# Folding squares ahead of the column sums and transposing 128x128 whole in a decoder trunk

## The chip, the cores and the metric

The kernel runs on one core of one Trainium2 chip. The metric is the device time of the whole program in microseconds (us). Three timed runs of the kernel before gave 1185.15, 1185.39 and 1186.02 us; their median is 1185.39 us.

## What is computed

One layer of a decoder trunk over 256 tokens of width 1024, float32: a mixer (sparse attention of 8 heads in 2 groups beside a short gated convolution), cross-attention to 256 memory rows, and a mixture of 32 experts. Cut to what the change touches:

```python
def compress_blocks(t, pos_emb, w1, b1, w2):          # t: keys or values, (B, S, G, 64)
    idx = jnp.arange(nc)[:, None] * CMP_STRIDE + jnp.arange(CMP_LEN)[None, :]
    blk = t[:, idx] + pos_emb[:, None, :]
    blk = jnp.moveaxis(blk, 3, 2).reshape(B, nc, G, CMP_LEN * dh)
    return jax.nn.gelu(blk @ w1 + b1) @ w2
...
sc = jnp.einsum('bsghd,bcgd->bghsc', qg, kc) * scale
p_cmp = jnp.where(cmask, masked_softmax(sc, cmask), 0.0)
o_cmp = jnp.einsum('bghsc,bcgd->bsghd', p_cmp, vc)
...
o = jnp.concatenate([rmsnorm(o_nsa, g_nsa_out), rmsnorm(o_conv, g_conv_out)], axis=-1)
return o @ w_mix_out
```

## The kernel before

The order of the work on each engine is written out by hand, with semaphores between the engines. The program has three stages. The first (to about 187 us) is the mixer. The second (to about 267 us) is the cross-attention and the router. The third runs through the 32 experts; each takes six loads of 2 MB of weights into a ring of 11 slots (line 497), 403 MB in all. The first 11 of these loads are gated one by one by steps of the second stage, because the slots hold data of the stages before; each later one waits until a slot is freed.

The mixer's middle is a loop over eight rounds n = 0 to 7: t = n // 4 is the half of the tokens, j = n % 4 a head of each group. In a round TensorE makes the scores (L1708), VectorE masks them and takes the maximum (`mask_max`, L1221 and L1222), ScalarE takes the exponentials (`exps`, L766), VectorE weighs them (`weigh`, L1228 to L1234), TensorE transposes them (`p_transposes`, by the helper `tr`, L1570) and ScalarE copies them out (`pt_out`, L777). Between these steps TensorE multiplies "units" (L1590 to L1592): chunks of the memory's keys and values, whose weights ScalarE (L655) and VectorE (L1024) have split into a high and a low part.

The steps of the change lie around and inside these rounds:

- `cmp_transposes` (L1684) turns the keys, then the values, of the compression into PSUM banks 6 and 4, before round 0. Each piece of 128 tokens by 64 columns is a multiplication by the identity, made twice so that both halves of the 128 partitions hold a copy. `blocks` (L1160, VectorE) reads them.
- `cmp_p_transposes` (L1799, round 3) turns the compressed probabilities `Pcf`, 16 pieces of 32 columns. `cmp_scores` and `cmp_weigh` on VectorE (L1195 to L1209) fill `Pcf`; `cmp_out` (L794, ScalarE) copies the result out; `pv(0)` (L1813, L1817) uses it in round 4.
- `column_sums` (L1728) sums squares `sq` over partitions by multiplying with a column of ones, four chunks for each half of the tokens. `conv_sums` runs in round 5, on squares that ScalarE writes before round 0 (L747). `o_sums` runs after the rounds, between `mix_out(0, 0)` and `mix_out(1, 0)` (L1826), on squares by `o_square` (L815). ScalarE takes its root (L857), and VectorE scales the attention's part into `H` with it (L1246).
- On GpSimd (POOL), `weight_low` (L573) makes the low part of the output weights in four pairs of subtractions, in rounds 4 to 7. After them the queue waits for the second stage (L586).

## Time and profile before

| what | value |
|---|---|
| median of three runs | 1185.39 us |
| span of the profiled execution | 1185.6 us |
| PE busy (multiplications) | 1117.9 us, 94% |
| PE weight loads | 498.0 us, 42% |
| VectorE, ScalarE, GpSimd busy | 319.6, 233.6, 36.3 us |
| moved by DMA | 445.50 MB, mean 376 GB/s |

No other time of the profiled execution than its span is given; the span lies within the spread of the three runs, so span and time are taken as the same here. A weight load (PEld) runs beside the multiplication before it, and each multiplication needs one, so the starts of the weight loads show the pace of TensorE; the ends of multiplications in the profile are modelled. A float32 multiplication shows as two instructions, a transposition through `tr` as one.

### The profile page before, as it was taken

To read this page: it belongs to the slowest core of one execution; us is meant where nothing else is said; L and a number is where in the kernel's file an instruction comes from. 1 tells how busy PE (TensorE), PEld (TensorE's weight loads), DVE (VectorE), ACT (ScalarE), POOL (GpSimd) and SP (SyncE) were. 2 spreads that over 40 slices of the span, in tenths; PEclk is the share of its full clock that TensorE was granted. 3 is DMA by queue.
4 is the path that set the end of the run, shared out by engine and by line. 5 is a ranking of instruction groups with operands and counts; after the bars stand their busy time and mean duration, and the time that the engine had idled before them with its cause. 6 is when DMAs were issued, how large, how long until landed. Compare 5 with 4: busy or idle time off the path is not lost.

```text
span 1185.6 us, 12841 instructions
## 1 busy us (share of the span) xinstructions
PE 1117.9 (94%) x5460; PEld 498.0 (42%) x5461; DVE 319.6 (27%) x719; ACT 233.6 (20%) x460; POOL 36.3 (3%) x35
## 2 busy tenths in 40 slices
PE   8999999999999999999999998999999989999896
PEld 7887678753333333333333333333333333333332
DVE  6787665233111111221111111111111111111112
ACT  6575665341100000110010000000000000000002
POOL 0000240220000000000000000000000000000000
PEclk9999999999999999999999999999999999999999
DMA  9915336769999999999999999999999999999995
GB/s 361 353 46 185 100 143 263 273 269 426 425 426 430 426 430 426 428 426 428 426 430 427 427 428 428 427 428 426 430 427 427 428 427 428 428 427 427 428 426 215
DMA packets 44586, 445.50 MB, mean 376 GB/s; under 512 B 6096, under 2 KB 10288, under 8 KB 19728
## 3 DMA queue, kind: packets, MB, share of 16 engines
q1 hardware_dynamic: 42784, 444.38, 90.0%
q8 instruction: 44, 0.72, 0.3%
q10 hardware_dynamic: 1744, 0.28, 0.1%
q14 instruction: 14, 0.11, 0.0%
HBM read 443.60 MB, written 1.05 MB: 375 GB/s over the span
## 4 chain that ended last, share of the span: by engine, by line
PE 59%; DMA 35%; DVE 2%; ACT 2%; issue 0%; SPq 0%; DVEq 0%; ACTq 0%
PE ps L2074 19%; DMA R<-in_w_gate_up 16%; PE ps L2083 11%; DMA R<-in_w_down 4%; DMA MK<-in_w_gate_up 4%; PE ps L1570 4%; DMA A<-in_w_gate_up 4%; DMA XMT<-in_w_gate_up 4%; DMA XM<-in_w_gate_up 4%; PE ps L2103 4%; PE ps L2050 3%; PE ps L1590 3%; PE ps L1592 3%; PE ps L1591 3%; PE ps L1934 2%; PE ps L1826 2%
## 5 line engine op out<-in xcount | busy, mean ns | idle before, releaser
L2074 PE MATMUL ps<-R,convT 128*64 128x512 f32 x1104 | 246.4, 594 | 17.4 <-DMA R<-in_w_gate_up 17.4
L1471 DVE TENSOR_SCALAR A<-ps 128x512 f32<-128x512 f32 x30 | 20.8, 692 | 645.1 <-PE ps L2074 645.1
L2074 PEld LDWEIGHTS ps<-R,convT 128*64 128x64 f32 x1104 | 76.7, 137 | 173.7 <-issue 135.7
L2083 PE MATMUL ps<-R,A 128*64 128x512 f32 x592 | 131.9, 593 | 2.2 <-DMA R<-in_w_down 2.2
L943 ACT ACTIVATE A<-A 128x512 f32<-128x512 f32 x30 | 18.9, 631 | 470.9 <-DVE A L1471 470.9
L2083 PEld LDWEIGHTS ps<-R,A 128*64 128x64 f32 x592 | 41.5, 137 | 79.7 <-issue 75.1
L2103 PE MATMUL ps<-A,convT 64*128 64x512 f32 x248 | 61.6, 615 | 1.4 <-ACT A L950 0.7
L950 ACT COPY A<-ps 128x512 f32<-128x512 f32 x30 | 17.6, 586 | 221.3 <-PE ps L2083 221.3
L2050 PE MATMUL ps<-H,convT 128*64 128x512 f32 x256 | 60.4, 593 | 0.1
L2074 PE MATMUL ps<-XMT,convT 128*64 128x512 f32 x208 | 46.9, 593 | 2.5 <-DMA XMT<-in_w_gate_up 2.5
L2065 PE MATMUL ps<-A,convT 96*64 96x512 bf16 x192 | 32.5, 388 | 15.4 <-ACT A L948 13.7
L2074 PE MATMUL ps<-MK,convT 128*64 128x512 f32 x192 | 43.4, 594 | 3.7 <-DMA MK<-in_w_gate_up 3.7
L2074 PE MATMUL ps<-QK,convT 128*64 128x512 f32 x192 | 43.4, 594 | 3.3 <-DMA QK<-in_w_gate_up 3.3
L1570 PEld LDWEIGHTS ps<-ident,A 128*128 128x128 f32 x272 | 35.3, 205 | 26.5 <-issue 23.3
L2074 PE MATMUL ps<-XM,convT 128*64 128x512 f32 x176 | 39.8, 594 | 4.5 <-DMA XM<-in_w_gate_up 4.5
L1570 PE MATMUL ps<-ident,A 128*128 128x128 f32 x272 | 41.6, 295 | 1.4 <-ACT A L974 0.7
L2074 PE MATMUL ps<-A,convT 128*64 128x512 f32 x176 | 39.7, 593 | 2.0 <-DMA A<-in_w_gate_up 2.0
L2103 PEld LDWEIGHTS ps<-A,convT 64*128 64x128 f32 x248 | 21.3, 186 | 41.3 <-issue 38.1
L1436 DVE TENSOR_TENSOR convT<-ps,prm 128x512 f32<-128x512 f32 x32 | 22.1, 692 | 46.0 <-PE ps L1570 46.0
L1592 PE MATMUL ps<-R_p,XM_p 128*128 128x512 f32 (+1 forms) x90 | 34.1, 378 | 0.0
L2050 PEld LDWEIGHTS ps<-H,convT 128*64 128x64 f32 x256 | 18.1, 137 | 36.4 <-issue 36.2
L948 ACT COPY A<-ps 128x512 f32<-128x512 f32 x30 | 17.6, 587 | 74.2 <-PE ps L1570 74.2
(323 smaller groups left out, 1290.3 us busy)
## 6 DMA issues: line engine op xcount, KB each, us to landing
R<-in_w_gate_up SPq DMA_DIRECT2D x69, 2048.0 KB, 45.5
R<-in_w_down SPq DMA_DIRECT2D x37, 2048.0 KB, 47.1
XMT<-in_w_gate_up SPq DMA_DIRECT2D x13, 2048.0 KB, 46.0
QK<-in_w_gate_up SPq DMA_DIRECT2D x12, 2048.0 KB, 47.2
MK<-in_w_gate_up SPq DMA_DIRECT2D x12, 2048.0 KB, 47.8
A<-in_w_gate_up SPq DMA_DIRECT2D x11, 2048.0 KB, 43.1
XM<-in_w_gate_up SPq DMA_DIRECT2D x11, 2048.0 KB, 46.9
XM<-in_w_down SPq DMA_DIRECT2D x6, 2048.0 KB, 38.6
```

Of the source, the lines that this page charges most:

```text
L1436: return V.tensor_tensor(dst, bank(U_BANK).rearrange("p (m n) -> p m n", m=KC), prm[:, R_XG:R_XG + KC].unsqueeze(2).to_broadcast([P, KC, S ...
L1570: return nc.tensor.transpose(dst, src, ident[0:k, 0:k])
L1590: mm(o, hi, whi, start=(kc == 0), stop=False)
L1591: mm(o, lo, whi, start=False, stop=False)
L1592: return mm(o, hi, wlo, start=False, stop=(kc == KC - 1))
L1826: last = mm(bank(MIX_BANKS[part][t][n]), a[:, c, t * P:(t + 1) * P], w[:, 4 * part + c, n * BANK:(n + 1) * BANK], start=(c == 0 and i == 0 ...
L1934: last = mm(bank(4 * t + 2 + n), lhs(c), w(c, n), start=(c == 0), stop=(c == KC - 1))
L2050: last = mm(bank(X_BANK)[s * SLOTS:(s + 1) * SLOTS, :], sel[:, t, :], H[:, t, s * BANK:(s + 1) * BANK], start=(t == 0), stop=(t == 1), ski ...
L2065: last = mm(bank(b)[s * SLOTS:(s + 1) * SLOTS, :], which, b_prt[:, at + s * BANK:at + (s + 1) * BANK], start=True, stop=False, skip_group_ ...
L2074: last = mm(bank(b)[s * SLOTS:(s + 1) * SLOTS, :], xg[:, 4 * (j % 2) + 2 * c + j // 2, :], w[:, c * 2 * FF + at + s * BANK:c * 2 * FF + at ...
L2083: last = mm(bank(o)[s * SLOTS:(s + 1) * SLOTS, :], h[:, c, i * SLOTS:(i + 1) * SLOTS], w[:, c * D + s * BANK:c * D + (s + 1) * BANK], star ...
L2103: last = mm(bank(Y_BANK + 2 * t + s), selT[s * SLOTS:(s + 1) * SLOTS, t * P:(t + 1) * P], orow[s * SLOTS:(s + 1) * SLOTS, :], start=False, ...
```

## The change

Three edits.

1. Keys and values of the compression are transposed whole, 128 tokens by both groups' 64 columns, by `tr`: two instructions for each of keys and values. There is one copy instead of two, with the group on the partitions; `blocks` reads a group's 64 partitions for both halves of its output.
2. `Pcf` is laid out by head first, so that four column blocks of 32 stand together, and is transposed by four whole `tr`.
3. GpSimd adds the four chunks of squares in two additions (128x512 and 128x256 elements for the convolution; 128x256 and 128x128 for each half of the attention), so that `column_sums` is one multiplication for each half. `conv_sums` waits for the fold before `weight_low` in GpSimd's queue; `o_sums` waits for the folds that stand behind all of `weight_low`.

```diff
@@ gpsimd
+                def fold_squares(x):
+
+                    link(nc.gpsimd.tensor_tensor(x[:, :, 0:2, :], x[:, :, 0:2, :], x[:, :, 2:4, :], ALU.add))
+                    nc.gpsimd.tensor_tensor(x[:, :, 0, :], x[:, :, 0, :], x[:, :, 1, :], ALU.add).then_inc(pool_sq, 1)
+
+                pool.wait_ge(act_cy, CC + 1)
+                fold_squares(sq)
                 i = 0
                 for n in range(T * J):
                     for _ in MIX_AT.get(n, []):
                         weight_low(i)
                         i += 1
+                for t in range(T):
+                    pool.wait_ge(act_osq, t + 1)
+                    fold_squares(sq[:, t:t + 1])
@@ vector
-                        rows = bank(6 - 2 * v)[i * HD:(i + 1) * HD, :].rearrange("p (g c m i) -> p g c m i", g=G, m=8, i=2)
                         for mh in range(2):
                             for g in range(G):
+                                rows = bank(6 - 2 * v)[g * HD:(g + 1) * HD, 0:S].rearrange("p (c m i) -> p c m i", m=8, i=2)
...
-                                    rows[:, g, mh:mh + NCMP, :, i],
+                                    rows[:, mh:mh + NCMP, :, i],
...
-                    pc4 = Pc.rearrange("p (g t j) c -> p g t j c", g=G, t=T)
+                    pc4 = Pc.rearrange("p (j g t) c -> p g t j c", g=G, t=T)
...
-                    c4 = csm[:].rearrange("p (g t j) -> p g t j", g=G, t=T)
+                    c4 = csm[:].rearrange("p (j g t) -> p g t j", g=G, t=T)
@@ tensor
                 def cmp_transposes(b, src):
-                    for g in range(G):
-                        for t in range(T):
-                            for i in range(2):
-                                last = mm(bank(b)[i * HD:(i + 1) * HD, g * S + t * P:g * S + (t + 1) * P],
-                                          src[:, t, 0, g * HD:(g + 1) * HD], ident[:], start=True, stop=True)
+                    for t in range(T):
+                        last = tr(bank(b)[:, t * P:(t + 1) * P], src[:, t, 0, :])
...
                 def column_sums(dst, t):
-                    for c in range(4):
-                        last = mm(dst, sq[:, t, c, :], ones[:, 0:1], start=(c == 0), stop=(c == 3))
-                    return last
+                    return mm(dst, sq[:, t, 0, :], ones[:, 0:1], start=True, stop=True)
 
                 def conv_sums():
                     pe.wait_ge(pool_cst, 5)
-                    pe.wait_ge(act_cy, CC + 1)
+                    pe.wait_ge(pool_sq, 1)
...
                 def o_sums():
-                    pe.wait_ge(act_osq, T)
+                    pe.wait_ge(pool_sq, 1 + T)
...
                 def cmp_p_transposes():
                     pe.wait_ge(dve_cp, 1)
-                    for g in range(G):
-                        for t in range(T):
-                            q = 32 * (2 * g + t)
-                            for j in range(J):
-                                a = (g * T + t) * J + j
-                                last = mm(bank(3)[q:q + 32, j * P:(j + 1) * P], Pcf[:, a * 32:(a + 1) * 32], ident[:],
-                                          start=True, stop=True)
+                    for j in range(J):
+                        last = tr(bank(3)[:, j * P:(j + 1) * P], Pcf[:, j * P:(j + 1) * P])
```

## Rows read from the trace of the kernel before

**Rows 1.** Busy time by stretch: PE, PEld, DVE, ACT, POOL, granted clock, DMA share, GB/s.

```profile
186.80:251.40 64.60, 63.56 (x266) 44.99 (x266) 18.92 (x30) 27.55 (x47) 13.90 (x12) 1.00 0.74 278
251.40:276.00 24.60, 23.15 (x119) 13.04 (x118) 12.79 (x47) 7.40 (x14) 0.00 (x0) 1.00 0.97 400
276.00:1125.00 849.00, 801.25 (x3840) 281.94 (x3838) 145.36 (x330) 71.75 (x120) 0.00 (x0) 1.00 1.01 427
```

**Rows 2.** Timeline of the load queue: start, length, engine, line, what, count.

```profile
186.86 0.99 SPq L488 DMA_DIRECT2D R<-in_w_xo  x2
...
251.44 0.33 SPq L497 DMA_DIRECT2D R<-in_w_gate_up  x1
```

**Rows 3.** Timeline of TensorE's weight loads; in brackets the idle time before.

```profile
77.48 0.86 PEld L1570 LDWEIGHTS ps<-ident,XM 128*128 128x128 f32 x8 [0.17 <-issue]
78.59 0.85 PEld L1684 LDWEIGHTS ps<-ident,QK 128*64 128x64 f32 x16 [0.26 <-ACT QK L743]
...
120.45 2.19 PEld L1799 LDWEIGHTS ps<-ident,R 128*32 128x32 f32 x32 [0.60 <-DVE R L1209]
...
130.05 0.20 PEld L1813 LDWEIGHTS ps<-R,QK 128*64 128x64 f32 x4 [0.36 <-issue]
...
134.80 1.87 PEld L1728 LDWEIGHTS ps<-ones,QK 128*128 128x128 f32 x16
137.47 0.19 PEld L1590 LDWEIGHTS ps<-R_p,XMT_p 128*128 128x128 f32 x1 [0.80 <-ACT A L757]
```

**Rows 4.** VectorE's timeline, rounds 0 to 4.

```profile
83.43 0.69 DVE L1221 SCALAR_TENSOR_TENSOR R<-ps,MK 128x512 f32<-128x512 f32 x1 [0.46 <-PE ps L1708]
...
119.99 0.41 DVE L1209 TENSOR_TENSOR R<-R,MK 128x240 f32<-128x240 f32 x1
...
122.25 0.68 DVE L1024 TENSOR_TENSOR A_p<-A,R_p 128x512 fp32r<-128x512 f32 x1
124.02 1.23 DVE L1221 SCALAR_TENSOR_TENSOR R<-ps,MK 128x1024 f32<-128x1024 f32 x1 [1.09 <-PE ps L1708]
```

**Rows 5.** ScalarE's timeline.

```profile
98.70 0.37 ACT L782 COPY R<-ps 128x256 f32<-128x256 f32 x1
...
128.52 0.62 ACT L777 COPY R<-ps 128x256 f32<-128x256 f32 x2
...
136.13 1.29 ACT L757 ACTIVATE A<-ps,rst 128x512 f32<-128x512 f32 x2
...
175.76 0.60 ACT L815 ACTIVATE QK<-ps 128x512 f32<-128x512 f32 x1 [1.19 <-DVE R_p L1242]
```

**Rows 6.** Busy time in a stretch of round 5, columns as in rows 1.

```profile
138.80:142.00 3.20, 3.20 (x9) 2.52 (x8) 1.81 (x2) 1.82 (x6) 3.20 (x2) 0.50 0.00 0
```

**Rows 7.** GpSimd's timeline.

```profile
1.22 0.29 POOL L554 TENSOR_SCALAR_AFFINE_SELECT ident<-ident 128x128 f32<-128x128 f32 x1 [0.23 <-POOL ident L553]
...
160.18 2.41 POOL L573 TENSOR_TENSOR R_p<-R,R_p 128x1024 fp32r<-128x1024 f32 x1 [0.62 <-ACT R_p L803]
...
162.54 2.45 POOL L573 TENSOR_TENSOR R_p<-R,R_p 128x1024 fp32r<-128x1024 f32 x1
```

**Rows 8.** VectorE's timeline around the weighing of rounds 6 and 7, and later.

```profile
151.24 1.14 DVE L1234 TENSOR_SCALAR R<-R,MK 128x256 f32<-128x256 f32 x4
...
160.32 2.42 DVE L1234 TENSOR_SCALAR R<-R,MK 128x256 f32<-128x256 f32 x1
...
162.66 3.00 DVE L1234 TENSOR_SCALAR R<-R,MK 128x256 f32<-128x256 f32 x3
...
177.00 1.41 DVE L1021 SCALAR_TENSOR_TENSOR A_p<-A,prm,R_p 128x512 fp32r<-128x512 f32 x2 [1.28 <-ACT R_p L653]
```

**Rows 9.** TensorE's weight loads at the last transposition of a round and at the attention's sums.

```profile
165.72 1.02 PEld L1570 LDWEIGHTS ps<-ident,R 128*128 128x128 f32 x8
...
178.22 1.99 PEld L1728 LDWEIGHTS ps<-ones,QK 128*128 128x128 f32 x16
...
180.13 0.30 PEld L1826 LDWEIGHTS ps<-R_p,XM_p 128*128 128x128 f32 x2
```

More of the change, by code:

```diff
@@ L343, in trunk @@
         act_part, pool_res = sem("act_part"), sem("pool_res")
+        pool_sq = sem("pool_sq")
         dve_seq, act_seq = sem("dve_seq"), sem("act_seq")
```

## The prediction

> **What bounds the kernel now.** I read the busy time by stretch first. From 276 to 1125 us the DMA share is 1.01 at 427 GB/s: the expert stage runs at the pace of its loads. From 186.8 to 251.4 us the share is only 0.74, and from 251.4 us on 0.97 and more [rows 1]. The load queue says why: its loads there are gated by TensorE's steps. The load of `w_xo` goes out at 186.86, when the mixer's output is done, and with the load at 251.44 the stream becomes full [rows 2]. So the end is the moment at which the stream becomes full plus a fixed amount of bytes. Between 186.9 and 251.4 us every gate is a TensorE step, so what the mixer saves on TensorE's path before 187 us passes to the end one for one, as long as it isn't eaten on the way. Nothing that the change does lies behind 187 us.
>
> Second, the timelines of the engines between 75 and 187 us. TensorE's weight loads follow each other with hardly a gap, but four waits matter: for ScalarE's L743 at 78.59, VectorE's L1209 at 120.45, ScalarE's L757 at 137.47 [rows 3], and the hidden copy L782 that ends at 99.07 [rows 5]. At these a saving made ahead of them on TensorE alone is lost unless the other engine gets earlier too. VectorE in turn waits for TensorE's scores 0.46 us at 83.43 and 1.09 us at 124.02 [rows 4].
>
> **Prices.** A whole transposition costs 0.86 / 8 = 0.11 us; 16 instructions of `cmp_transposes` cost 0.85, the 32 of `cmp_p_transposes` 2.19, the 16 of the sums 1.87, which is 0.117 each [rows 3], and 1.91 at the second place (178.22 to 180.13) [rows 9]. A GpSimd addition isn't in the trace; the nearest is the subtraction of 128x1024 elements at 2.41 us [rows 7]. In proportion 512, 256 and 128 columns are 1.2, 0.6 and 0.3 us; with a fixed part up to 0.4 us each (the smallest GpSimd operation shown, 128x128, is 0.29 in all) they are at most 1.6, 1.0 and 0.7. I take 0.1 us above the low ends, since the step between the two subtractions, 2.36 us, leaves little room for a large fixed part. The handover between the two additions is 0.23 us [rows 7].
>
> **Keys** (16 instructions to 2, 0.85 to 0.22): worth nothing. What follows already waits 0.26 us for ScalarE's L743 at 78.59 [rows 3], the last of ScalarE's own queue of copies.
>
> **Values** (16 to 2): 0.85 - 0.22 = 0.63, plus the 0.17 us issue gap that follows such a group (as ahead of 77.48), 0.8 us on TensorE [rows 3]. VectorE is busy until 82.97 and waited only 0.46 us for the scores of round 0 [rows 4], so it gets 0.46. From there it works without a gap through round 0 to the exponentials of round 1, whose ScalarE queue holds the copy L782 that TensorE waits for [rows 5]. So 0.46 is what is left at 99 us: TensorE's other 0.3 us becomes a longer wait there. `blocks` has as many instructions with as many elements as before: 0.
>
> **Probabilities** (32 to 4): 2.19 - 0.43 = 1.76 us, directly behind VectorE's L1209, which ends at 120.40 and moves by 0.46. TensorE gets 0.46 + 1.76 = 2.22. Next in line: VectorE ends L1024 at 122.93 and then waits 1.09 for the scores of round 4 [rows 4], so it gets 0.46 + 1.09 = 1.55 and waits no more. Its chain leads to the copies L777, which end at 129.14 and `pv(0)` needs; now 127.59 [rows 5]. TensorE comes to `pv(0)` at 130.05 - 2.22 = 127.83 [rows 3], just behind them. So 2.22 passes, and `pv(0)` hands it to ScalarE, which waits for it before L757. At 137.47 all of it is still there.
>
> **Sums of the convolution** (16 to 4, 1.87 to 0.47): nothing. TensorE waits 0.80 us for L757 behind them [rows 3, 5]; that wait becomes 2.2 us. Their fold on GpSimd runs from about 81.5 to 84 us in an idle queue, 48 us ahead of its use, and `weight_low` behind it starts only at 138: 0, with that cover.
>
> **The clock.** Behind that wait TensorE's granted clock falls: 0.50 from 138.8 to 142.0 [rows 6], the lower of its two levels (1.2 against 2.4 GHz). In 3.2 us at half pace it loses 1.6 us. Ahead of it came 1.87 us of one-column multiplications and 0.80 us of idling; with the change it is 0.47 and 2.2 us, together again 2.67 us without dense work. I take the fall as unchanged: 0; if it goes, another 1.6 us are gained, if it comes twice, 1.6 are lost.
>
> **The fold of the first half** stands behind the eighth `weight_low`, which ends at 164.99 [rows 7]. The trace shows a price: the four weighings of round 7 took 5.34 us, against 1.14 in round 6. The first took 2.42 beside the subtraction of 160.18, the other three together 3.00, most of it beside the one from 162.54 [rows 7, 8]. A GpSimd operation that reads memory holds these VectorE operations until it ends. They end at 165.66 and TensorE's transposition starts at 165.72 [rows 8, 9]: no slack at all. Now the fold's first addition (0.7 us from 165.0) holds the third weighing, where before the last two ran freely. The fourth slips into the 0.23 us handover. That is +0.4 us; if the second addition holds the fourth one too, and with the high prices, +1.4. If VectorE wins both times, 0. I take 0.4.
>
> **Sums of the attention** (16 to 4): 1.91 - 0.47 = 1.44 us, on the path: behind them `mix_out(1, 0)` runs on without a wait [rows 9]. The new wait: `o_square` ends at 176.36 [rows 5]; handover 0.2, additions 0.7 + 0.23 + 0.4 give 177.9, against TensorE's arrival at 178.22 [rows 9]: hidden by 0.3 us. VectorE's L1021 at 177.00 [rows 8] may hold an addition by up to 0.7. I take +0.1; bounds 0 and +1.2 (high prices and the hold). TensorE queues `mix_out(1, 0)` behind this wait, and the root, the scaling of `H` and the load at 186.86 wait for it.
>
> The Trainium skill, "SBUF — State Buffer", section "Who interferes with whom", says that VectorE and GpSimd share a port pair which one takes for a whole instruction, and that VectorE instructions with two inputs in SBUF contend as well. The first half agrees with the 5.34 us above; no row here shows the second. By that rule L1021, which reads two such inputs, blocks or is blocked by the fold of the second half.
>
> **Sum**: 0.46 + 1.76 + 0 - 0.4 + 1.44 - 0.1 = 3.16 us off 1185.6. The span lies 0.2 us above the median of the runs, so I take the 3.1 off the median: **1182.3 us**.
>
> **The rivals.**
> (A) The forecast, 1182.3.
> (B) The locks between GpSimd and VectorE take the high ends: 1.4 at the weighings of round 7 and 1.2 at the sums. Then 0.46 + 1.76 - 1.4 + 1.44 - 1.2 = 1.1, which gives 1184.3, no measurable change. For it: there is no slack at 165.72 and 0.3 us at 178.22. Against: both need the high price of a small addition. The skill's rule on two inputs is a way to it, for the sums alone: the 0.7 of L1021 less 0.3 of slack, 1182.7.
> (C) The clock doesn't fall: 3.1 + 1.6 = 4.7, 1180.7.
> (D) It falls for twice as long, or once more at the wait for L782: 3.1 - 1.6 = 1.5, 1183.9.
> (E) Slower. The pairs of subtractions lie close to the weighings: in round 6 these start at 151.24 [rows 8]. If the shifts of the engines differ, so that two rounds' weighings lie beside a pair as those of round 7 do, each takes 5.34 - 1.14 = 4.2 us more. Before TensorE needs them there are about 1.4 us in round 5 and 1.1 in round 6, so 2.8 + 3.1 = 5.9 lost against 3.1 won: 1188.2. It decides from 3.1 us of holding beyond the cover. Against it: both are set off by the same ScalarE queue and move together.
>
> **How the numbers follow.** A 0.45, B 0.22, C 0.13, D 0.08, E 0.12. A measurement here can tell about 0.2%, 2.4 us, from no change. A and C are faster: 0.58; B and D within: 0.30; E slower: 0.12. The range from 1180.2 to 1185.2 takes in A to D with their bounds and leaves out E and the outer tails.
>
> **What would show it.** In the profile after: 4 loads in place of the 32 of L1799 and no wait of VectorE before the scores of round 4; `pv(0)` about 2.2 us earlier; a wait of 2 us for L757; the stretch at half clock as long as before; the third weighing of round 7 held, and its transposition late by some 0.4 us; four loads of the attention's sums without a wait; the first `w_xo` load at 183.8 and the 251.44 load at 248.3. It is wrong if the saving at the first `w_xo` load isn't found at the end, which would mean that loads and not TensorE gate the second stage, or if TensorE waits for GpSimd over 1 us.

## The result: slower, by a branch that costs 6 us and a gain eaten on VectorE

The changed kernel takes 1194.35 us (median of 4 runs, 1193.73 to 1194.83), the kernel before beside it 1185.70 (4 runs): a ratio of 1.0067, interval 1.0055 to 1.0079, so 8.7 us slower. The forecast was 1182.3, faster. The profiled execution of the changed kernel has a span of 1192.0 us and took 1193.73. Each timed run gives its span too, and the time is 1.7 to 2.1 us above it. So the profiled execution before (span 1185.6) took about 1187.4 us, some 1 to 2 us above the medians of its kernel. I had taken span and time as the same. I compare stretches below, and medians for the end.

**Up to 187 us: next to nothing gained.** TensorE's weight loads after, the same places as in [rows 3] and [rows 9]:

```profile
77.42 0.86 PEld L1581 LDWEIGHTS ps<-ident,XM 128*128 128x128 f32 x8 [0.64 <-ACT XM L749]
78.87 0.20 PEld L1581 LDWEIGHTS ps<-ident,QK 128*128 128x128 f32 x2 [0.59 <-ACT QK L754]
...
101.21 0.52 PEld L1769 LDWEIGHTS ps<-R 128*128 128x128 f32 x4 [2.18 <-ACT R L793]
...
122.56 0.42 PEld L1581 LDWEIGHTS ps<-ident,R 128*128 128x128 f32 x4 [0.61 <-DVE R L1220]
...
130.37 0.20 PEld L1814 LDWEIGHTS ps<-R,QK 128*64 128x64 f32 x4 [0.37 <-ACT R L788]
...
135.12 0.53 PEld L1735 LDWEIGHTS ps<-ones,QK 128*128 128x128 f32 x4
137.78 0.19 PEld L1601 LDWEIGHTS ps<-R_p,XMT_p 128*128 128x128 f32 x1 [2.13 <-ACT A L768]
...
166.76 0.86 PEld L1581 LDWEIGHTS ps<-ident,R 128*128 128x128 f32 x8 [0.81 <-DVE R L1245]
...
179.40 0.52 PEld L1735 LDWEIGHTS ps<-ones,QK 128*128 128x128 f32 x4 [0.34 <-POOL QK L582]
```

Each group shrank as forecast: 0.85 to 0.20, 2.19 to 0.42, 1.87 to 0.53, 1.99 to 0.52. But the transposition of the probabilities starts at 122.56, where it was 120.45: 2.1 us late instead of 0.46 early. The place where it got late is on VectorE:

```profile
81.15 3.26 DVE L1171 TENSOR_TENSOR R<-ps,prm 64x120 f32<-64x120 f32 x8
84.44 0.69 DVE L1232 SCALAR_TENSOR_TENSOR R<-ps,MK 128x512 f32<-128x512 f32 x1
...
87.10 3.23 DVE L1171 TENSOR_TENSOR R<-ps,prm 64x120 f32<-64x120 f32 x8
```

These are the 16 copies of `blocks`. Before, they took 1.2 and 1.1 us less:

```profile
80.87 2.09 DVE L1160 TENSOR_TENSOR R<-ps,prm 64x120 f32<-64x120 f32 x8
...
86.08 2.15 DVE L1160 TENSOR_TENSOR R<-ps,prm 64x120 f32<-64x120 f32 x8
```

The mask of round 0 starts at 84.44, where it started at 83.43 after a wait for TensorE [rows 4]; now it comes when VectorE itself is free.

**The load queue**, as in [rows 2]:

```profile
186.60 0.99 SPq L489 DMA_DIRECT2D R<-in_w_xo  x2
...
251.18 0.33 SPq L498 DMA_DIRECT2D R<-in_w_gate_up  x1
...
1133.60 0.33 SPq L538 DMA_DIRECT2D QK<-in_w_down  x1
```

The third of them before:

```profile
1126.05 0.33 SPq L537 DMA_DIRECT2D QK<-in_w_down  x1
```

The first two are 0.26 us early, both. The third, the load of the last half, is 7.55 us late: from 251 us, where it is 0.26 ahead, to 1134 us the kernel loses 7.8 us. The DMA rate between is the same, 427 to 428 GB/s.

**At 1121 us.** TensorE's weight loads there, after; line 2104 is `scatter` at the end of an expert, line 2066 the bias of the next expert:

```profile
1120.79 0.19 PEld L2104 LDWEIGHTS ps<-A,convT 64*128 64x128 f32 x2 [0.23 <-issue]
1127.09 0.22 PEld L2066 LDWEIGHTS ps<-A,convT 96*64 96x64 bf16 x4 [6.11 <-issue]
```

Before, at the same place:

```profile
1121.00 0.19 PEld L2103 LDWEIGHTS ps<-A,convT 64*128 64x128 f32 x2 [0.24 <-issue]
1121.95 0.14 PEld L2065 LDWEIGHTS ps<-A,convT 96*64 96x64 bf16 x4 [0.76 <-issue]
```

After, TensorE stands for 6.1 us, and what it waits for is no engine and no transfer of data ("issue"). Between the two lines of code there is only a value load, the test `pe.If(more > 0)`, and a jump over a loop for more tokens than this input has. The jump has a record of its own in the trace (it isn't counted as busy). Before it started at 1120.91 and took 0.46 us, after at 1120.71 and took 6.25 us. Neither the test nor the loop is touched by the change. TensorE's clock also falls, first while it stands; busy time by stretch, columns as in rows 1:

```profile
1120.00:1130.00 10.00, 4.69 (x18) 1.77 (x20) 0.00 (x0) 0.00 (x0) 0.00 (x0) 0.76 1.01 428
1130.00:1140.00 10.00, 10.00 (x44) 3.44 (x42) 0.00 (x0) 0.00 (x0) 0.00 (x0) 0.90 1.00 423
1140.00:1150.00 10.00, 8.15 (x43) 3.52 (x40) 4.40 (x9) 1.80 (x3) 0.00 (x0) 0.95 1.02 433
1150.00:1160.00 10.00, 10.00 (x44) 3.51 (x42) 0.00 (x0) 0.00 (x0) 0.00 (x0) 0.88 0.99 419
```

Before, all four stretches have 1.00. After, the clock's records in the trace show two falls to half: from 1125.1 to 1131.9 us, which began some 4 us into the stand, and from 1149.0 to 1152.4. TensorE works in 4.8 and 3.4 us of them, so it loses 4.1 us of full-speed work. With the 5.8 us of the jump that is 9.9 us. The end moves by 8 to 8.7 us, so some 2 us of it are taken up by waits that were there before.

### The profile page after: what moved, and what is told of

The parts are those of the page before. It is cut to its first block, busy times and chain, and to the rows that moved or that the text cites. A ratio compares the mean times of both kernels' runs of the same rounds, so it can differ in the third digit from the quotient of the medians.

```text
span 1192.0 us, 12687 instructions
## 1 busy us (share of the span) xinstructions
PE 1116.9 (94%) x5380; PEld 494.9 (42%) x5381; DVE 322.2 (27%) x719; ACT 233.3 (20%) x460; POOL 41.0 (3%) x41
## 3 DMA queue, kind: packets, MB, share of 16 engines
HBM read 443.60 MB, written 1.05 MB: 373 GB/s over the span
## 4 chain that ended last, share of the span: by engine, by line
PE 61%; DMA 31%; DVE 4%; ACT 2%; issue 1%; DVEq 0%; ACTq 0%
PE ps L2075 21%; DMA R<-in_w_gate_up 15%; PE ps L2084 12%; PE ps L1581 4%; DMA A<-in_w_gate_up 4%; DMA MK<-in_w_gate_up 4%; DMA XMT<-in_w_gate_up 4%; PE ps L2104 4%; DMA XM<-in_w_gate_up 4%; PE ps L2051 3%; PE ps L1601 3%; PE ps L1602 3%; PE ps L1603 3%; PE ps L1935 2%; PE ps L2066 1%; PE ps L1827 1%
```

## The theory of the jump

TensorE's instructions are loaded too. The page after has the row

```profile
q8 instruction: 43, 0.70, 0.2%
```

43 packets in 0.70 MB are 16 KB each, and in steady work one comes every 256 instructions that TensorE executes. I counted the instructions of each kernel in order (two for a whole transposition, a bfloat16 or a float32r multiplication, four for a float32 one, one for a wait). Before, the branch is the 10583rd and its target the 10864th; after, 10423rd and 10704th: the three edits take 56 + 56 + 48 = 160 instructions away ahead of it. The traces hold 10575 and 10415 records of TensorE ahead of the branch, 8 short of the count in both and 160 apart. The jump is over 281 instructions in both, but it lies at 87 from a multiple of 256 before and at 183 after. The theory: one packet ahead of the running one is loaded, and a jump that lands beyond it waits for a load. The times fit: before, one packet started at 1111.8, nine microseconds ahead of the branch; after, the last ahead of it started at 1091.7, the next only at 1124.5, 3.8 us into the stand, and TensorE runs again at 1127.0.

The Trainium skill, "Runtime: NRT & Kernel Launch", section "Instruction fetch mechanics", has the rule: instructions come in blocks of 16 KiB one after the other, and "a taken branch whose target isn't in the current 2-page window forces a DMA fetch of the target page before execution can continue". I had not weighed that page, since the change doesn't touch a branch. Its price is not in it; the trace gives 5.8 us.

The rival: the change delays the end otherwise (GpSimd, the transfers, the clock), and the branch only shows it.

## Experiments on the jump

The tool for all of these is a wait that is long fulfilled, repeated at the head of an expert's TensorE part. Two such waits make one instruction, and TensorE has some slack in each expert. For e1, e2, f4, h3, h4 and i1 only the counts differ:

```diff
@@ tensor, def expert(k)
+                    for _ in range(8 if 1 <= k <= 20 else 0):
+                        pe.wait_ge(m_bsel, k + 1)
                     bias(G_BANK, 0, bsel)
```

**e1: the changed kernel, 80 instructions more.**

> The changed kernel, with 8 more fulfilled waits (4 instructions, two waits each) on TensorE at the head of each of the experts 1 to 20: 80 instructions more ahead of the branch over the conditional block, and no work more; TensorE has some 2 us of slack in each expert. Theory (code placement): the branch costs 6.25 us in the changed kernel because of where it lies in the code, which is loaded in packets of 16 KB (256 instructions): the branch is at instruction 10423 (183 from the last multiple of 256), its target 281 instructions on. With 80 more it lies at 7 from a multiple, so the branch takes some 0.5 us, the last experts run at a granted clock of 1.00, and the time is that of before within 1.5 us (1184.5 to 1187.0). Rival (something the change does to the engines, the transfers or the clock delays the end): placement is nothing, the branch still takes some 6 us, 1193 to 1195.

Measured: 1187.03 us (10 runs), just at the upper end of the expected, ratio to before 1.0008 (0.9999 to 1.0018). The branch takes 0.46 us. Its weight loads:

```profile
1120.39 0.19 PEld L2104 LDWEIGHTS ps<-A,convT 64*128 64x128 f32 x2 [0.23 <-issue]
1121.34 0.14 PEld L2066 LDWEIGHTS ps<-A,convT 96*64 96x64 bf16 x4 [0.76 <-issue]
```

Eighty instructions that do nothing take 8 us off the changed kernel (it was 8.65 above its runs of before, now 0.68).

**e2: the kernel before, 96 instructions more.**

> The kernel before, none of the change in it, with 12 more fulfilled waits (6 instructions) on TensorE at the head of each of the experts 1 to 16: 96 instructions, so that its branch (at 10583, 87 from a multiple of 256) lies at 10679, 183 from a multiple: just where the changed kernel has it. Theory (code placement): the branch takes some 6 us, the clock dips behind it, and the time rises by 7 to 9 us to 1192.5 to 1195. Rival (the change itself): branch some 0.5 us, 1185.2 to 1186.7.

Measured: 1190.98 us (4 runs), ratio 1.0045 (1.0029 to 1.0060). The branch takes 6.37 us:

```profile
1120.08 0.19 PEld L2103 LDWEIGHTS ps<-A,convT 64*128 64x128 f32 x2 [0.24 <-issue]
1126.49 0.21 PEld L2065 LDWEIGHTS ps<-A,convT 96*64 96x64 bf16 x4 [6.22 <-issue]
```

The stand is there without any of the change. The time rises by 4.6 us only, less than expected. Here the clock falls once, from 1123.2 to 1130.0 us, and half of that lies within the stand; TensorE loses 1.8 us by it:

```profile
1120.00:1130.00 10.00, 4.58 (x18) 1.55 (x16) 0.00 (x0) 0.00 (x0) 0.00 (x0) 0.66 0.99 419
1130.00:1140.00 10.00, 10.00 (x50) 3.62 (x48) 0.00 (x0) 0.00 (x0) 0.00 (x0) 1.00 1.01 428
```

and it stays at 1.00 to 1160 us, where the changed kernel has the end of its longer loss and the second fall. The changed kernel loses 2.3 us more by the clock, out of the 3.4 by which e2's rise falls short of 8.0. This is not one execution alone: the timed runs of the changed kernel have a mean granted clock of 0.989 to 0.993, those of e2 0.995 to 0.997. Why the clock falls again in the one and not in the other these runs don't tell.

**f4: the kernel before, 84 more.**

> The kernel before, with 12 fulfilled waits (6 instructions) at the head of each of the experts 1 to 14: branch at 10667, 171 from a multiple of 256, target 196 from one. Theory: the target is missed when two borders of 256 instructions lie between branch and target, which are 281 apart, so for a band of 25 places only; 183 is inside, 239, 7 and 87 are outside. The borders as the sequencer counts them then lie between 184 and 208 in my count, and 171 is in the band if they lie at 196 or below: branch 6 us. Otherwise 0.5 us, and the border lies between 197 and 208. Rival (no such band; any place from about 100 to 230 is dear): 6 us.

Measured: 1194.06 us (one run). The branch itself takes 0.37 us, and yet TensorE stands, one weight load later. The group of TensorE's multiplications behind the target:

```profile
1127.32 1.06 PE L2065 MATMUL ps<-A,convT 96*64 96x512 bf16 x4 [5.04 <-issue]
```

The first weight load of that group is at 1122.20 in the records, its multiplication at 1127.32. So the border lies between them: ahead of instruction 10950, which is 198 from a multiple of 256 in my count. The target, 10948, was there; what followed wasn't. My "6 us or 0.5 us at the branch" was too coarse: entering the last instructions of a packet is as dear as missing it.

**h3: the kernel before, 60 more.** With the border known, a number can be forecast.

> The kernel before with 60 instructions of fulfilled waits ahead of its branch: branch at 10643, 147 from a multiple of 256, target at 10924. In the run with 84 the first weight load behind the target (10949) ran and the next instruction (10950) came 5.1 us later, so a border lies at 10950, 198 from a multiple of 256 in my count. Theory (one packet is loaded ahead, and the next is asked for only when the branch has jumped into it, arriving 6.15 us after the branch): target is 26 instructions ahead of the border; TensorE runs the 4 short and 8 or 9 of the long multiplications of the expert and then waits 2.5 to 3.1 us, about 3.2 us after the branch. Rival (a miss is all or nothing): no wait there, or 5 us at the branch.

Measured: 1188.54 us (one run), the branch 0.37 us. TensorE's multiplications:

```profile
1121.30 0.62 PE L2065 MATMUL ps<-A,convT 96*64 96x512 bf16 x4
1121.75 1.89 PE L2074 MATMUL ps<-QK,convT 128*64 128x512 f32 x8
1126.26 3.29 PE L2074 MATMUL ps<-QK,convT 128*64 128x512 f32 x8 [2.62 <-issue]
```

It stops after the 4 short and 8 long ones, as forecast, and for 2.62 us. The records show nine weight loads of the long ones, the ninth of them instruction 10949: the same border. The price of a jump is thus the time of a load, 6 us, less the work that stands between target and border.

**h4: the kernel before, 116 more.**

> The kernel before with 116 instructions of fulfilled waits ahead of its branch: branch at 10699, 203 from a multiple of 256, just behind the border at 198. Theory: the target (228 in the next) is in the packet loaded ahead and has 226 instructions to its border: no wait, 0.5 us for the branch, time as before. Rival (late in its 256 is dear): 6 us.

Measured: 1192.35 us (one run), and the branch takes 6.46 us. The theory missed this one: only one border lies between branch and target. But the branch stands 5 instructions behind the border at 10694, and both stand behind `scatter`'s wait, which ended at 1120.3. So the packet with the target was asked for less than 1 us before the jump. No packet started between 1089.9 and 1125.2. The one at 1125.2 comes 4.0 us behind the start of the branch, as in the changed kernel and e2 (both 3.8), so the jump rather than the border seems to have asked for it; that isn't shown.

**i1: the kernel before, 138 more.**

> The kernel before with 138 instructions of fulfilled waits ahead of its branch: branch at 10721, 27 behind the border at 10694; the run with 116 had it 5 behind the border and its branch took 6.46 us, the run of edits 2 and 3 had it 41 behind and took 0.37 us. The sequencer passes the border at the latest with the last multiplications ahead of scatter, some 2.6 us before the branch. Theory A (the packet that is under way serves the jump): the branch takes at most 3.6 us, or the wait comes as short as that. Theory B (a jump into a packet still under way asks anew and pays in full): 6.2 to 6.5 us. Theory C (the packet is there by then, the sequencer being further ahead than that): 0.4 us.

Measured: 1186.37 us (one run), the branch 0.48 us. A packet started at 1117.05, 4.5 us ahead of the branch. With 27 instructions between border and branch the border lies ahead of `scatter`'s wait, and TensorE's sequencer had passed it long before. It is theory C of the expectation, and the time is that of before. Whether a packet under way would serve the jump stays open.

All together, by the place of the branch (target 281 further, borders at 198):

| kernel | branch, mod 256 | instructions from target to the next border | branch | TensorE stands | lost at half clock behind it | time less before |
|---|---|---|---|---|---|---|
| e1 | 7 | 166 | 0.46 us | no | | +0.7 (10 runs) |
| before | 87 | 86 | 0.46 | no | | |
| h3 | 147 | 26 | 0.37 | 2.6 us, 26 on | 1.7 us | +2.2 (1 run) |
| f4 | 171 | 2 | 0.37 | 5.0 us, 2 on | 4.2 | +7.3 (1 run) |
| after | 183 | beyond it | 6.25 | at the branch | 4.1 | +8.7 |
| e2 | 183 | beyond it | 6.37 | at the branch | 1.8 | +4.6 |
| h4 | 203 | 226, but the border just passed | 6.46 | at the branch | 1.7 | +6.0 (1 run) |
| i1 | 225 | 204 | 0.48 | no | | -0.2 (1 run) |
| e4 (below) | 239 | 190 | 0.37 | no | | |

The loss at half clock is half of the time that TensorE works in the falls of the clock between 1120 and 1160 us. In h3, f4 and h4 the time rises by the stand plus this loss, less about 2 us (1.7 to 2.1), and in the changed kernel too, measured against e1; in e2 by 3 us less. So the clock behind the stand is two fifths of what the jump costs the changed kernel. (e4 has a fall at 1139 us too, without a stand.) From about 130 (an estimate: the work of some 50 instructions fills 6 us at h3's pace) to beyond 203 of 256 places it costs something. That the kernel before stood at 87 and the changed one at 183 is chance.

## Experiments on the edits

Edits 1 to 3 move the branch as well; e4, f1, f2 and f3 stand at 239, 31, 31 and 39, all cheap, so they need no padding.

**e4: edits 2 and 3, without edit 1.**

> Edits 2 and 3 alone (whole transposes for the probabilities, folds on GpSimd); keys and values are transposed, and the blocks copied, as before. No padding: the branch is at 10479, 239 from a multiple of 256. Theory: the two groups of 8 copies take 2.1 us each as before, nothing of VectorE's chain is late, so the mixer ends 1.5 to 2.7 us earlier than before (first load of the cross-attention's output weights at 184.2 to 185.4), and the branch takes some 0.5 us, since at 239 one multiple of 256, not two, lies between the branch and its target: 1182.5 to 1184.5. If the rule of the placement is only that any branch late in its 256 instructions is dear, the branch takes 6 us here, and the time is 1190 to 1192.

Measured: 1183.93 us (10 runs), ratio 0.9979 (0.9970 to 0.9989): 2.4 us faster, within the expected range of the time. VectorE's copies and the load queue:

```profile
81.23 2.14 DVE L1171 TENSOR_TENSOR R<-ps,prm 64x120 f32<-64x120 f32 x8
...
86.44 2.15 DVE L1171 TENSOR_TENSOR R<-ps,prm 64x120 f32<-64x120 f32 x8
```

```profile
183.68 1.66 SPq L489 DMA_DIRECT2D R<-in_w_xo  x2
...
248.25 0.33 SPq L498 DMA_DIRECT2D R<-in_w_gate_up  x1
```

The loads are 3.2 us earlier than in [rows 2], nearly the places that the forecast named for the whole change, and 0.5 us earlier than the early end of the expectation. Some 0.9 us of this is the clock: this run has no fall at 136 to 144 us, as e2 (1.00 there, `w_xo` at 185.93) has none and before (0.50 for 3.2 us [rows 6], 186.86) has one.

**f1, f2, f3: each edit alone.**

> Edit 1 alone (whole transposes of keys and values; blocks copied in the order of the change). Branch at 10527, 31 from a multiple of 256, so cheap (0.5 us). Theory (VectorE sets the pace between the scores of round 0 and the exponentials of round 1): the 1.1 us that TensorE saves become a wait, the two groups of 8 copies take 3.25 us instead of 2.1 each, and hidden_transposes start 2 us later than before; with that idle time TensorE's clock falls at least as often as before. 1.5 to 3.5 us slower than the kernel before. Rival (the transposes' saving outweighs it, and what e1 lost against e4 came from the clock alone): within 0.8 us of before.

> Edit 2 alone (four whole transposes of the probabilities). Branch at 31 from a multiple: cheap. Theory, as forecast: TensorE's 16 multiplications (2.19 us) become four of one instruction (0.42), and 1.76 us go from a stretch in which TensorE has no gaps: 1.3 to 2.0 us faster than before, first load of the cross-attention's output weights 1.3 to 2.2 us earlier. Rival (pv(0) waits for ScalarE's copy, or VectorE sets the end): 0 to 0.8 us.

> Edit 3 alone (squares folded on GpSimd). Branch at 39 from a multiple: cheap. Theory: the attention's sums save 1.45 us of TensorE, the convolution's 1.34 us fall into a wait that was there; the fold of the first half beside VectorE's weighing in round 7 makes that 0.75 us longer and p_transposes(7) waits 0.8 us. Net 0.6 to 1.0 us faster than before. Rival (the folds on GpSimd hold up VectorE or ScalarE also elsewhere): 0.5 us faster to 1 us slower.

Measured, 11 runs each, before 1186.76: edit 1 alone 1188.82, ratio 1.0019 (1.0010 to 1.0028), 2.1 us slower; edit 2 alone 1184.54, 0.9984 (0.9975 to 0.9993), 2.2 us faster; edit 3 alone 1185.71, 0.9991 (0.9982 to 1.0000), 1.05 us faster, at the edge of what can be told. Edit 1 is within its expected range, edits 2 and 3 just beyond theirs; that the clock would fall at least as often with edit 1 failed, since f1's profile has no fall in the mixer. Starts differ by up to 1 us from run to run before the edits act, so I take two intervals: from the first copy of `blocks` to the first `w_mix_out` load, and from there to the first `w_xo` load.

| kernel | blocks to `w_mix_out` | `w_mix_out` to `w_xo` | clock fall at 136 to 144 |
|---|---|---|---|
| before | 30.90 | 75.09 | yes |
| e2 (before, padded) | 30.91 | 74.17 | no |
| f1, edit 1 | 32.68 | 74.10 | no |
| f2, edit 2 | 30.86 | 73.39 | yes |
| f3, edit 3 | 30.88 | 74.20 | yes |
| e4, edits 2 and 3 | 30.90 | 71.55 | no |
| after, all | 32.71 | 72.74 | yes |

The mixer of before also runs in four more of the profiles: with the fall 75.12, 75.15 and 75.11 us in the second interval (f4, h4, i1), without it 74.11 (h3). So one profile of each kernel tells about a tenth of a microsecond here.

Edit 1 costs 1.8 us in the first interval and changes nothing in the second. Edits 2 and 3 change nothing in the first; in the second, compared at the same clock, edit 2 gives 1.70, edit 3 gives 0.89, both 2.62. The fall costs 0.9. For the change: 2.35 gained less 1.81 lost, 0.5 us over both intervals.

**e3: why the copies of `blocks` got slower.** In the records each of the 8 lasts 0.36 to 0.40 us before and after, but before they start 0.22 us apart (0.41 only where the loop goes to the other half of the partitions), after always 0.40 to 0.43. After, each copy reads other partitions than the one before it, since the group is now on the partitions and is the innermost loop.

```diff
                     for i in range(2):
-                        for mh in range(2):
-                            for g in range(G):
+                        for g in range(G):
+                            for mh in range(2):
```

> The changed kernel with the 80 instructions of padding and, in VectorE's copies of the compression's blocks, the loop over the groups outside the loop over the halves of 8 rows. Theory (partition change): two such copies in a row start 0.22 us apart when both read and write the same partitions as the one before, 0.40 us apart when either changes; the changed kernel changes the source at each of 8 copies, this order at 3 of 8. So the 8 take 0.37 + 4 x 0.22 + 3 x 0.40 = 2.45 us instead of 3.26, both times, and the mixer ends 0.8 to 1.6 us earlier than that of the changed kernel: first load of the cross-attention's output weights at 185.0 to 185.8. Time 1183.5 to 1185.5 if the branch is cheap, too. Rival (shifted partitions are slow as such): the pairs that read other partitions than they write stay 0.40 us apart, 5 of 8 copies, 2.8 us. Rival to the placement theory: 1192 to 1194.

Measured: 1186.00 us (11 runs), ratio 0.9996 (0.9987 to 1.0005). The first eight copies (the second eight took 2.53 us):

```profile
81.02 2.46 DVE L1171 TENSOR_TENSOR R<-ps,prm 64x120 f32<-64x120 f32 x8
```

2.46 us against an expected 2.45, and 2.8 for the rival: it is the change of partitions from one instruction to the next that costs, not a copy to other partitions as such. The Trainium skill, "VectorE: DVE Perf Modes", section "Two Vector instructions with no wait between them", says just that: by its model, an instruction whose input or output starts in another group of 32 partitions than that of the one before it starts only when all earlier ones have finished. The trace agrees, 0.40 against 0.22 us. In the profile the rest of the expectation failed: `w_xo` was loaded at 186.69, no earlier, though the time is near the expected. The profile has a fall of the clock that e1's profile doesn't have. It comes behind this wait, which is 2.18 us in e1:

```profile
99.59 0.52 PEld L1769 LDWEIGHTS ps<-R 128*128 128x128 f32 x4 [2.19 <-ACT R L793]
```

In the stretch from 100 to 104 us the granted clock is 0.57 here and 1.00 in e1; with 4 us at 0.57 that is 1.7 us of the work of TensorE. From e1 to e3 the median falls by 1.0 us all the same, and e1's profiled run was its fastest (1185.36). Compared at the same mean granted clock the order of the copies is worth more: at 0.995 the four runs of e1 took 1187.2 to 1188.2 us, the seven of e3 1186.0 to 1186.5; at 0.998 e1 took 1185.4 and 1185.6, e3 1184.3. So it is 1.2 to 1.8 us, if falls of the clock cost the same wherever they lie.

**h1: what the fold costs VectorE.** After, the four weighings of round 7 (L1245) took 6.09 us at 160.62, where they took 5.34 [rows 8], and `p_transposes(7)` waits 0.81 us for them. The fold of the first half stands behind `weight_low` at 165.24, though its squares are ready 15 us earlier. In h1 (edits 2 and 3) it moves ahead:

```diff
@@ gpsimd
                         weight_low(i)
                         i += 1
-                for t in range(T):
-                    pool.wait_ge(act_osq, t + 1)
-                    fold_squares(sq[:, t:t + 1])
+                    if n == 5:
+                        pool.wait_ge(act_osq, 1)
+                        fold_squares(sq[:, 0:1])
+                pool.wait_ge(act_osq, T)
+                fold_squares(sq[:, 1:2])
```

> Edits 2 and 3, and the fold of the attention's first half moved on GpSimd from behind the last four subtractions of weight_low to the gap after the first four (round 5: its squares are ready at 150.1, the queue is idle from 149.7 to 152.9). Theory (the fold holds up VectorE's weighing in round 7): that group takes 5.3 us again instead of 6.1, p_transposes(7) wait 0.1 us or less instead of 0.8, and the first load of the cross-attention's output weights comes 0.5 to 0.9 us earlier against a run of edits 2 and 3 with the same clock: 183.0 or so. Time 2.4 to 3.8 us below the kernel before. Rival (the lengthening came from the subtractions of weight_low): group still 6.0 us, time as of edits 2 and 3 alone, 1.8 to 3.0 below before.

Measured: 1182.75 us (6 runs), ratio 0.9969 (0.9957 to 0.9980), 3.6 us faster than before. VectorE's weighings in e4 and here:

```profile
157.89 6.08 DVE L1245 TENSOR_SCALAR R<-R,MK 128x256 f32<-128x256 f32 x4
```

```profile
158.72 5.33 DVE L1247 TENSOR_SCALAR R<-R,MK 128x256 f32<-128x256 f32 x4
```

The 0.75 us are the fold's, and the wait of 0.81 us is gone. One by one, the third weighing took 0.82 us after and 0.34 before, the fourth 0.61 and 0.34: both are held. In the profiled run `w_xo` is nevertheless at 183.96 against e4's 183.68, because this one has the fall of the clock (0.81 from 136 to 144 us) and e4 has not. From `w_mix_out` to `w_xo` it takes 71.77 us against e4's 71.55; less 0.9 for the fall it is 0.7 us shorter.

**h2, i3: relieving VectorE.** If VectorE sets the pace at 81 to 99 us, 0.58 us less on it must come through whole. On top of h1, the memset and the two additions of the identity (L1286 to L1290) are taken out there and go to GpSimd ahead of round 0:

```diff
@@ gpsimd
                 nc.gpsimd.memset(Pcf, 0.0).then_inc(pool_cst, 1)
+                link(nc.gpsimd.memset(fold, 0.0))
+                for v in range(2):
+                    nc.gpsimd.tensor_tensor(fold[:, v, 0:2 * NCMP], ident[:, 32 * v:32 * v + 2 * NCMP],
+                                            ident[:, 64 + 32 * v:64 + 32 * v + 2 * NCMP], ALU.add).then_inc(pool_cst, 1)
@@ tensor
-                    pe.wait_ge(dve_blk, 19)
+                    pe.wait_ge(pool_cst, 9)
```

> As the run with the fold in round 5, and three small operations of VectorE (a memset and two additions of the identity, 0.58 us with their gaps, between conv_low and the mask of round 1) are done by GpSimd ahead of round 0. Theory (VectorE without a gap from 81 to 97 us sets when ScalarE's exponentials of round 1 and hidden_transposes start): the wait of hidden_transposes falls from 0.98 to 0.4 to 0.5 us, w_xo's load comes up to 0.5 us earlier, time up to 0.5 us below that run. Rival (another wait takes its place at once): nothing.

> The kernel of h2 once more, beside the mended three edits on the same chip: 2.6 to 4.2 us below the kernel before, from blocks to w_mix_out's load 30.4 us.

Measured: 1182.89 us (10 runs, 0.9974, 0.9964 to 0.9983) and in a second set 1183.24 (11 runs, 0.9974, 0.9965 to 0.9983). From blocks to `w_mix_out` 30.38 and 30.42 us instead of 30.90: 0.5 us, as expected; the wait of `hidden_transposes` falls from 0.98 us to 0.62 and 0.59. The median shows nothing of it against h1: 0.5 us is below what these runs tell apart.

**i2: all three edits, mended**: the order of e3, the fold of h1, the identity of h2, and 80 instructions of padding.

> All three edits, with the copies of the blocks by group outside the halves of 8 rows, the fold of the first half in round 5, the identity's sums on GpSimd, and 80 instructions of padding (branch at 10503, 7 from a multiple of 256: cheap). Theory (edit 1 buys nothing even when it is mended, since VectorE and not TensorE sets the pace at 81 to 99 us): against the kernel without edit 1 the copies take 0.74 us more, from blocks to w_mix_out's load 31.0 to 31.3 us instead of 30.4, and TensorE waits 1 us longer at hidden_transposes: 0.2 to 1.5 us slower than that kernel, 1183 to 1184.5. Rival (TensorE's saving of 1.1 us shows once VectorE is relieved): 0.3 to 1.0 us faster than that kernel.

Measured: 1184.10 us (8 runs), ratio 0.9975 (0.9965 to 0.9986), beside i3's 1183.24. From blocks to `w_mix_out` 30.83 against 30.42, less apart than expected. TensorE at `hidden_transposes`:

```profile
99.54 0.52 PEld L1769 LDWEIGHTS ps<-R 128*128 128x128 f32 x4 [1.76 <-ACT R L799]
```

and in i3:

```profile
99.51 0.52 PEld L1772 LDWEIGHTS ps<-R 128*128 128x128 f32 x4 [0.59 <-ACT R L799]
```

What edit 1 saves on TensorE, 1.2 us, is waited for in full, and the first interval is 0.4 us longer.

The second interval of i2 is longer too: 71.92 us against 71.03 in h2, both without the fall. This comes from the attention's sums:

```profile
171.00 1.34 ACT L670 ACTIVATE R_p<-A,prm 128x512 fp32r<-128x512 f32 x2 [5.26 <-DMA A<-in_w_xq]
```

```profile
176.92 0.52 PEld L1735 LDWEIGHTS ps<-ones,QK 128*128 128x128 f32 x4 [1.04 <-POOL QK L586]
```

ScalarE waits for the load of `w_xq`; its `o_square`, and with it the fold of the second half, stands behind that, and TensorE waits 1.04 us for the fold. In h2 ScalarE waits less and TensorE not at all:

```profile
171.61 1.34 ACT L670 ACTIVATE R_p<-A,prm 128x512 fp32r<-128x512 f32 x2 [4.01 <-DMA A<-in_w_xq]
```

In the four kernels with all three edits (after, e1, e3, i2) this load takes 14.0 to 14.2 us to land, in the thirteen others 12.8 to 13.3. Only in those four does a packet of TensorE's instructions start within the load, 6.2 to 6.6 us behind its issue. So the shift of the instructions seems to cost up to 1 us here as well. No run moves this packet alone, so the cause is argued and not shown; and of what edit 1 costs in i2, only the 0.4 us of the first interval are surely its own.

So mended, edit 1 gains nothing: 0.4 us lost in the first interval, 0.9 in the medians. All three edits, with the two accidents mended and with the help of h1 and h2, are 2.5 us faster than the kernel before. Without edit 1 the same help gives more: the best kernels are h1 and h2, 3.6 and 3.5 us below the medians beside them.

## Why the prediction was wrong, step by step

- **"Nothing that the change does lies behind 187 us": wrong, and the largest miss.** 160 fewer instructions on TensorE lie ahead of a jump at 1121 us. Shown by e1 and e2: 8.0 and 4.6 us. In its place the runs show a stand of 6 us at the jump and, behind it, up to 4 us lost at half clock, less 2 us of slack. No rival had it.
- **"`blocks` has as many instructions with as many elements as before: 0": wrong.** 3.26 and 3.23 us instead of 2.09 and 2.15, +2.25 us on a chain that I had myself called gapless. Shown by e3 for the cause and f1 for the price, 2.1 us at the end.
- **Values, 0.46: wrong in effect.** The step reasoned rightly that VectorE has only 0.46 us to give; the copies took 1.0 us away at the same place, so the scores of round 0 came early for nothing. i2 shows that with the copies mostly mended (2.47 and 2.55 us) nothing is left either: TensorE waits 1.76 us for ScalarE where i3 waits 0.59.
- **Keys, 0: right.** The wait for ScalarE at that place grew from 0.26 to 0.59 us, and a second one, 0.64 us for L749, stands ahead of it.
- **Probabilities, 1.76: right** in size (f2: 1.70 at the same clock, 2.2 in the median). `pv(0)` came not 2.2 us early but 0.3 late (130.37), because VectorE's lateness stood ahead of it; there it waits 0.37 us for ScalarE's copy, as the step had it "just behind".
- **Sums of the convolution, 0: right.** Their 1.87 us became 0.53, the wait behind them 2.13 us for 0.80; "2.2" was the forecast. The fold took 1.3 + 0.7 us in an empty queue.
- **The clock unchanged, 0: right for the profiled run** (0.50 from 138.8 to 142.0 again), but it isn't a property of the kernel. e2, e4, f1 and h3 lack the fall, and the mixers of e2 and h3 are that of before. It is worth 0.9 us, not the 1.6 that I worked out from 3.2 us at half pace. Of the rest, 0.5 us are waits: at its next two transpositions TensorE waits 0.94 and 1.08 us for VectorE in e2, and stands 0.76 us each before.
- **Fold of the first half, -0.4 (0 to -1.4): the mechanism right, the size 0.75**, the two additions 0.78 and 0.46 us. The step let the fourth weighing slip into a handover of 0.23 us; the handover took 0.08 us, and the fourth was held for 0.27. Shown by h1. That it was put where it hurts, and could be moved for nothing, the prediction did not see.
- **Sums of the attention, +1.44, less 0.1 for the wait: the saving right, the wait by another way.** 1.99 to 0.52 us, and a wait of 0.34 us for GpSimd. The step took `o_square` at 175.76; after, it starts at 177.04, since ScalarE waits longer for `w_xq`. In e4 and f3, where that load isn't late, TensorE doesn't wait. VectorE's L1032 beside the fold took 1.62 us instead of 1.41, and the fold's second addition 0.82 instead of 0.46. So the rule of the Trainium skill, "SBUF — State Buffer", section "Who interferes with whom", on VectorE instructions with two inputs in SBUF, for which I had no row, agrees with this trace: 0.2 and 0.4 us. Edit 3 in all: 1.44 - 0.1 - 0.4 = 0.9 forecast, 0.89 measured at the same clock. That these agree so well is luck in part: the fold cost more and the wait less than forecast, and small gains of some 0.3 us (the last transposition of the rounds takes 0.86 us instead of 1.02, for one) were not in the sum.
- **What is saved at the `w_xo` load passes to the end one for one: about right.** In e4 the loads at 183.68 and 248.25 are 3.2 us early and the branch at 1118.26 is 2.65 us early.
- **Span as time: wrong by 1.8 us**, without effect, since I took the saving off the median.

In numbers: forecast -3.1; of that the edits 2 and 3 are -2.7 forecast and -2.4 measured (e4), edit 1 -0.5 forecast and +2.1 measured (f1), which gives -0.3, against +0.7 of e1, whose interval (0.9999 to 1.0018, -0.1 to +2.1 us) comes within 0.2 us of it, and which has 0.4 us of waiting for the late `w_xq` in it; the jump 0 forecast and +8.0.

## What to carry to other kernels

Where an engine jumps over code it doesn't need, each instruction taken out or put in ahead of the jump moves it against the borders of 256 instructions. Look at the longest single wait by "issue" in both traces, and move the branch by some dozens of idle instructions before an edit is judged. Compare runs at the same granted clock. When a layout moves an index onto the partitions, look at the order of the instructions that read it: keep the partitions the same from one to the next, and set the saving of the engine ahead against the chain that really has no gaps.

## What the runs showed of the hardware

- A jump to instructions that aren't loaded costs TensorE 5.8 to 6.0 us beside a full DMA stream, of which 3.8 to 4.0 pass before the packet starts. A jump into the end of a packet costs the same less the work up to the border (2.6 us at 26 instructions, 5.0 at 2). One shortly behind a border (5 instructions, with a wait ahead of both) costs 6.0 us.
- The borders were at 198 from a multiple of 256 in my count from the kernel's first instruction, in two kernels alike.
- VectorE starts small copies (64 x 120 elements, 0.38 us each) every 0.22 us on the same partitions and every 0.40 us when either operand changes to the other half.
- One and the same kernel has or hasn't a fall of TensorE's clock at one place of the mixer, worth 0.9 us at `w_xo`; this is a good part of the spread of 2 to 3 us between its runs. A stand of 6 us came with one fall of the clock to half in two kernels (e2, h4: 1.8 and 1.7 us lost) and with a second one 24 us later in two others (after, f4: 4.1 and 4.2 us lost).
- A load of 4 MB beside which a packet of TensorE's instructions started took 14.0 to 14.2 us, without it 12.8 to 13.3 (four and thirteen kernels; that the packet is the cause isn't shown).
